# Latent attention heads: value products in high and low parts, and a new order of the work around them

## The chip, the cores and the metric

One core of a Trainium2 chip runs the whole program. The metric is device time in microseconds (us); the profile is of one execution on that core. The core's engines work from queues of their own, in order, and wait for one another on semaphores: TensorE (matmul, PE, with its weight loads as PEld), VectorE (DVE), ScalarE (ACT), GpSimd (POOL), and SyncE (SP), which issues most transfers.

## The reference, cut to what matters

A first block (a mixer with recurrence and convolution, then a feed-forward part) is followed by a second block of two attention layers. The change is in the first of these, latent attention over 512 tokens and 256 context tokens with 16 heads:

```python
q = (rms_norm(q_lat, g_qa) @ w_qb).reshape(bsz, n, A_HEADS, A_NOPE + A_ROPE)      # 64 + 32
kv = (rms_norm(kv_lat, g_kva) @ w_kvb).reshape(bsz, n, A_HEADS, A_NOPE + A_V)     # 64 + 64
q_pe, k_pe = apply_rope(q_pe, cos, sin), apply_rope(k_pe, cos, sin)
# a token attends to tokens and context, a context token to the context
s = jnp.einsum('bqhgd,bkhd->bhgqk', q, k) * scale
p = jax.nn.softmax(s, axis=-1)
o = jnp.einsum('bhgqk,bkhv->bqhgv', p, v)
out = o.reshape(gate.shape) * jax.nn.silu(gate)     # then @ out_w, residual, layer norm
```

Everything is float32.

## The kernel before

Weights come as a stream of blocks of 16 tiles (128 x 128) into two raw buffers. GpSimd's `split` (L719, L732) turns each block into a high part (type float32r, which TensorE takes in one pass) and a low part (what is left), in four parts; a product is then three passes: high x high, high x low, low x high. A raw buffer and its parts serve every second block. The activations are split in the same manner, high parts by a ScalarE copy, low parts by a VectorE subtraction.

The heads run from about 850 to 1106 us. A head has seven steps, `j` = 0 to 6: six for the 128 keys each of the 768 (scores of 512 queries), and step 6 for the context queries. In step `j` TensorE issues, in this order: from step 5 on `row` of the next head (once), the scores of the *next* step (L1394 and L1397, three passes), one product of five for the next head's maxima (`tops`, L1364, L1365, L1368), a piece of the projection of the head after next (`query` at steps 0 and 2; `key` at step 4 of even heads; `value_tokens` at steps 4 and 5 of odd heads, serving a pair), and the value product of *this* step (L1415, L1418). This last one is in plain float32, weights `Pf` by values `VV`. A block of ones beside the 64 value columns gives the softmax's sums in the other 64 rows of the same output.

VectorE takes a maximum (`top`, L2967) of each `tops` product; the next `tops` waits for it, since the output buffer is single. The five give a row that is subtracted inside the score product: `row` puts it across, ScalarE's `row_copy` writes it into `QHI`, and the next head's scores wait for it. Between the maxima VectorE has the rotary part of the query (`rope_query`, `rope_query_sum`, L2951), the low parts (`query_lo` L2955, `key_lo` L2961), and `inverse` (L2978), reciprocals of 256 columns of the sums, three for a pair of heads: one in the even, two in the odd head after the pair. GpSimd's `finish` then divides a pair's outputs (L788) and multiplies by the gate (L790), with a weight block's `split` after every second pair.

ScalarE's queue in a head: output of the head before (`output_x`, after the first exponential `output_c`), the exponentials (`weigh_keys`, L2156), the query's copy behind step 3, its high part (`query_hi`, L2125) behind step 4; in even heads the key's high parts (`key_hi`, L2131), one behind step 5 and one behind step 6, with `row_copy` between; in odd heads the values' copy at the end. In head 15 the high parts of the gated output (`out_high`, L2176) stand between the exponentials, and VectorE's `out_low` (L3018) follows. The first query product of an odd head waits for `key_lo`, as both use the output buffer `wide(2)`. Behind the heads comes the output projection (`residual_product`), which takes its eighth input only when the last pair is divided, gated and split.

Of the kernel before, what the change touches and what calls it, by code (L numbers as in the profile page):

```python
# [114 lines left out]
def build(nc, x_t, ctx_t, stream, ada_w, vectors, squares, level_masks, scan_mask, ropes, lora_w, gate_w,  # L115
# [289 lines left out]
    QHI = [reg(f"QHI{i}", [P, TA], kb, F32R) for i, kb in enumerate((136, 67, 73))]  # L405
    QLO = [reg(f"QLO{i}", [P, TA], kb, F32R) for i, kb in enumerate((139, 70, 76))]
    KHI = [[reg(f"KHI{i}{e}", [P, TA], kb + 3 * e, F32R) for e in range(2)] for i, kb in enumerate((115, 79))]
    KLO = [[reg(f"KLO{i}{e}", [P, TA], kb + 3 * e, F32R) for e in range(2)] for i, kb in enumerate((121, 85))]
    VV = [[reg(f"V{i}{e}", [P, 6, P], kb + 3 * e) for e in range(2)] for i, kb in enumerate((127, 100))]
    qf = [reg("qf0", [P, TA], 133), reg("qf1", [P, TA], 46)]  # L410
    Pf = reg("Pf", [P, 4, T], 106)
    Of = [reg("Of0", [P, TA], 91), reg("Of1", [P, TA], 40)]
# [4 lines left out]
    OT_HI = [reg(f"OT_HI{k}", [P, TA], kb, F32R) for k, kb in enumerate((49, 52, 55, 58, 61, 64, 67, 100))]  # L417
    OT_LO = [reg(f"OT_LO{k}", [P, TA], kb, F32R) for k, kb in enumerate((70, 73, 76, 79, 85, 97, 91, 103))]
    rope = at("rope", [P, 2, T], F32, tmp_at)
# [19 lines left out]
    score_full, value_done, tops_full = sem("score_full"), sem("value_done"), sem("tops_full")  # L439
    qproj_full = sem("qproj_full")  # L440
    exp_done, query_copied, query_high = sem("exp_done"), sem("query_copied"), sem("query_high")
    value_copied, ox_copied, oc_copied = sem("value_copied"), sem("ox_copied"), sem("oc_copied")
# [63 lines left out]
    def value_signal(p):  # L506

        if p == N_PAIRS - 1 or (p and p % 2 == 0):
            return block_done, pair_block(p)[0] + 1
        return vproj_full.at((p + 1) // 2 + 1 if p else 1)  # L510

    def nope_rows(e):
# [201 lines left out]
    def _(pool):  # L714
# [69 lines left out]

        def finish(p):

            pool.wait_ge(sums_inverse, 3 * p + 3)
            pool.tensor_tensor(Of[p % 2][:, :], Of[p % 2][:, :], Ls[p % 2][:, :], ALU.mult).then_inc(pair_divided, 1)  # L788
            pool.wait_ge(pair_divided, p + 1)
            pool.tensor_tensor(gate_s[:, p, :], gate_s[:, p, :], Of[p % 2][:, :], ALU.mult).then_inc(pair_out, 1)  # L790
# [11 lines left out]
        for e in range(2):  # L802
            c = slice(96, 128) if e == 0 else slice(0, 32)
            step(pool.memset(KHI[1][e][c, :].bitcast(F32), 0.0))
            step(pool.memset(KHI[1][e][top_at(e):top_at(e) + 1, :].bitcast(F32), 1.0))
            step(pool.memset(KLO[1][e][c, :].bitcast(F32), 0.0))
            step(pool.memset(VV[1][e][:, :, 64 - 64 * e:128 - 64 * e], 1.0))
        pool.sem_inc(mla_filled.sem, 1)
# [4 lines left out]

        n = before
        for p in range(N_PAIRS):
            finish(p)
            if p % 2 == 0:
                split(n, half_of(n), n // 2)
                n += 1
        if n % 2:  # L820
            split(n, 1, n // 2)
        rest, third = n + n % 2, STREAM["diff_out"] + 2
# [15 lines left out]
    def _(pe):  # L838
# [465 lines left out]
        def query(h, k):  # L1304

            p, e = h // 2, h % 2
            n, t0 = pair_block(p)
            if k == 0:
                pe.wait_ge(split_full, n + 1)
                if h == 1 or (e == 0 and h > 0):  # L1310
                    pe.wait_ge(value_copied, max(p, 1))
                if h == 2:
# [65 lines left out]
        def scores(h, j):  # L1378
# [12 lines left out]
            for k, q, first, last in ((KHI, QHI, True, False), (KHI, QLO, False, False), (KLO, QHI, False, True)):  # L1391
                kt, qq = k[p % 2][e], q[h % 3]
                if j < 6:
                    mm = pe.matmul(banks[i % 2][:, :], kt[:, P * j:P * j + P], qq[:, 0:T], start=first, stop=last)  # L1394
                else:
                    for c in range(2):
                        mm = pe.matmul(banks[i % 2][:, C * c:C * c + C], kt[:, T + P * c:T + P * c + P], qq[:, T:TA],  # L1397
                                       start=first and c == 0, stop=last and c == 1, skip_group_check=True)
            mm.then_inc(score_full, 1)

        def values(h, j):
# [12 lines left out]
            if j < 6:  # L1414
                mm = pe.matmul(pairs[1][:, 0, :], v[:, j, :], Pf[:, i % 4, :], start=(j == 0), stop=(j == 5), skip_group_check=True)  # L1415
            else:
                for c in range(2):
                    mm = pe.matmul(pairs[1][:, 1, 0:C], v[:, 4 + c, :], Pf[:, i % 4, C * c:C * c + C], start=(c == 0), stop=(c == 1),  # L1418
                                   skip_group_check=True)
# [36 lines left out]
        for h in range(A_HEADS):  # L1456
            nxt, after = h + 1, h + 2
            for j in range(N_S):
# [8 lines left out]
                if after < A_HEADS:  # L1467
# [275 lines left out]
    def _(act):  # L1743
# [391 lines left out]
        def value_copy(p):  # L2135
# [3 lines left out]
            for e in range(2):  # L2139
                c = slice(64 * e, 64 * e + 64)  # L2140
                ins = act.activation(VV[p % 2][e][:, :, c], wide(2).rearrange("p (a b) -> p a b", a=6)[:, :, c], ACT.Copy)
            ins.then_inc(value_copied, 1)
# [8 lines left out]
        def weigh_keys(h, j):  # L2151
            i = N_S * h + j
            act.wait_ge(score_full, i + 1)
            if i >= 4:
                act.wait_ge(value_done, i - 3)
            act.activation(Pf[:, i % 4, :], banks[i % 2][:, :], ACT.Exp, scale=A_SCALE).then_inc(exp_done, 1)  # L2156

        def take_output(h, n, cols, src, done):

            p, e = h // 2, h % 2  # L2160
            mine, sums = nope_rows(e), nope_rows(1 - e)
            act.wait_ge(value_done, n)
            if p >= 2:
                act.wait_ge(pair_out, p - 1)
            act.activation(Of[p % 2][mine, cols], src[mine, :], ACT.Copy)
            act.activation(Ls[p % 2][mine, cols], src[sums, :], ACT.Copy).then_inc(done, 1)
# [22 lines left out]
        for h in range(A_HEADS):  # L2189
# [14 lines left out]
            if h == A_HEADS - 1:  # L2204
                out_high(1)
            weigh_keys(h, 3)
            if h == A_HEADS - 1:
                out_high(2)
            if after < A_HEADS:
                query_copy(after)  # L2210
            weigh_keys(h, 4)
            if after < A_HEADS:
                query_hi(after)
# [3 lines left out]
            if h == A_HEADS - 1:  # L2217
                out_high(4)
            if after < A_HEADS and h % 2 == 0:
                key_hi(after // 2, 0)  # L2220
# [227 lines left out]
    def _(dve):  # L2448
# [481 lines left out]
        for e in range(2):  # L2930
            c = slice(96, 128) if e == 0 else slice(0, 32)
            dve.memset(KHI[0][e][c, :].bitcast(F32), 0.0)
            dve.memset(KLO[0][e][c, :].bitcast(F32), 0.0)
            ins = dve.memset(VV[0][e][:, :, 64 - 64 * e:128 - 64 * e], 1.0)
        chain.link(ins)
# [17 lines left out]
        def query_lo(h):  # L2953
            dve.wait_ge(query_high, h + 1)
            dve.tensor_tensor(QLO[h % 3][:, :], qf[h % 2][:, :], QHI[h % 3][:, :], ALU.subtract).then_inc(query_low, 1)  # L2955

# [25 lines left out]
        key_lo(0)  # L2982
        query_lo(0)
        rope_query(1)
        rope_query_sum(1)
# [4 lines left out]
        for h in range(A_HEADS):  # L2990
            nxt, after = h + 1, h + 2
            if nxt < A_HEADS:
                top(nxt, 0)
            if h >= 2:
                inverse((h - 2) // 2, 0 if h % 2 == 0 else 1)
            if nxt < A_HEADS:
                top(nxt, 1)
            if h >= 2 and h % 2:
                inverse((h - 2) // 2, 2)
            if nxt < A_HEADS:  # L3000
                top(nxt, 2)
            if after < A_HEADS:
# [7 lines left out]
            if after < A_HEADS:  # L3010
                query_lo(after)
                if h % 2 == 0:
                    key_lo(after // 2)
        def out_low(k):
            dve.wait_ge(ot_hi, k + 1)
            if k == KT - 1:
                dve.wait_ge(value_done, N_S * A_HEADS)
# [558 lines left out]
```

## Time and profile before

| | |
|---|---|
| median of 3 runs | 1634.55 us (1633.47 to 1636.34) |
| profiled execution | 1634.97 us, its span 1633.2 us |
| TensorE busy | 1569.9 us (96%) |
| VectorE, GpSimd, ScalarE busy | 996.3, 922.8, 695.8 us |
| granted TensorE clock, mean | 0.995 of full speed |
| heads | about 850 to 1106 us |

A matmul's recorded length is longer than the time it costs, since matmuls overlap; what one costs is the distance from its start to the next start. Behind a float32 product the records of starts run ahead, so distances are taken over a whole group.

### The profile page before, as it was taken

Reading aid. Unit: us, or ns where it says so; the run is one execution under the profiler, and the core shown is the slowest. Engines: PE = TensorE matmul, PEld = TensorE weight load, DVE = VectorE, ACT = ScalarE, POOL = GpSimd, SP = SyncE. Lnnn points to the kernel's source line nnn. Section 1 sums busy time; section 2 is a strip of 40 time slices with the busy share of each in tenths; the row PEclk is TensorE's granted clock in tenths of the full one; section 3 lists DMA queues with packets and bytes.
Section 4 is the critical chain, followed back from the end, with each engine's and each line's share of the span. In section 5 each row is a group of like instructions: output and inputs, shape, how many; then the busy total and the mean of one; then the engine's idle time right before and its main releaser. Section 6 shows DMA issues by size and latency. Waiting matters only on the chain.

```text
span 1633.2 us, 27294 instructions
## 1 busy us (share of the span) xinstructions
PE 1569.9 (96%) x11080; PEld 1272.0 (78%) x11080; DVE 996.3 (61%) x1315; ACT 695.8 (43%) x1210; POOL 922.8 (57%) x735
## 2 busy tenths in 40 slices
PE   8999888999999999989999999999999999999996
PEld 7677887678888888877877777768878888888775
DVE  6699886747555640044455766664676665666666
ACT  5552775333222220042246555563263344444563
POOL 5344887929999999965471312326624443344522
PEclk9999999999999999999999999999999999999998
DMA  6121104422332233231110000004231101111201
GB/s 206 70 103 52 55 4 159 155 104 78 103 103 84 96 141 142 103 142 69 61 58 21 27 0 27 0 1 155 84 137 52 46 33 52 52 52 52 116 40 52
DMA packets 20605, 126.08 MB, mean 77 GB/s; under 512 B 2288, under 2 KB 4592, under 8 KB 6416
## 3 DMA queue, kind: packets, MB, share of 16 engines
q1 hardware_dynamic: 20352, 124.02, 21.1%
q8 instruction: 79, 1.29, 0.3%
q10 hardware_dynamic: 144, 0.52, 0.1%
q14 instruction: 30, 0.25, 0.0%
HBM read 122.43 MB, written 2.10 MB: 76 GB/s over the span
## 4 chain that ended last, share of the span: by engine, by line
PE 77%; DVE 10%; issue 7%; ACT 3%; POOL 2%; DMA 0%; SPq 0%; POOLq 0%; ACTq 0%; DVEq 0%
PE banks L873 7%; PE banks L874 7%; PE banks L875 6%; PE banks L1415 5%; PE banks L1626 4%; PE banks L1629 4%; PE banks L1627 4%; PE banks L1394 4%; PE banks L1277 3%; PE banks L1282 3%; PE banks L1278 3%; PE banks L1249 2%; PE banks L1248 2%; PE banks L1250 2%; PE banks L1681 2%
## 5 line engine op out<-in xcount | busy, mean ns | idle before, releaser
L732 POOL TENSOR_TENSOR w_hi<-raw,der 128x512 fp32r<-128x512 f32 x296 | 333.8, 1138 | 399.9 <-PE banks L1629 203.5
L719 POOL TENSOR_TENSOR w_lo<-raw,w_hi 128x512 fp32r<-128x512 f32 x336 | 476.6, 1431 | 59.2 <-ACT w_hi L1782 58.9
L873 PE MATMUL banks<-h_hi,w_hi 128*128 128x512 f32 x464 | 184.2, 397 | 0.3 <-DVEq L2502 0.3
L874 PE MATMUL banks<-h_lo,w_hi 128*128 128x512 f32 x464 | 180.7, 389 | 0.0
L875 PE MATMUL banks<-h_hi,w_lo 128*128 128x512 f32 x464 | 180.6, 389 | 0.0
L1626 PE MATMUL banks<-h_hi,w_hi 128*128 128x512 f32 (+1 forms) x384 | 145.8, 380 | 1.3 <-DVE h_lo L3083 1.3
L1627 PE MATMUL banks<-h_lo,w_hi 128*128 128x512 f32 (+1 forms) x384 | 130.8, 355 | 0.0
L2307 ACT ACTIVATE dP<-banks,der 128x768 f32<-128x768 f32 x60 | 54.1, 902 | 159.0 <-DVE der L3181 159.0
L1629 PE MATMUL banks<-h_hi,w_lo 128*128 128x512 f32 (+1 forms) x384 | 115.9, 356 | 0.0
L788 POOL TENSOR_TENSOR Of<-Of,Ls 128x768 f32<-128x768 f32 x8 | 14.7, 1832 | 173.0 <-DVE Ls L2978 173.0
L873 PEld LDWEIGHTS banks<-h_hi,w_hi 128*128 128x128 f32 x464 | 87.1, 188 | 25.8 <-issue 7.5
L3181 DVE TENSOR_REDUCE der<-banks 128x1 f32<-128x768 f32 x64 | 60.9, 953 | 70.9 <-PE banks L1662 70.9
L874 PEld LDWEIGHTS banks<-h_lo,w_hi 128*128 128x128 f32 x464 | 87.1, 188 | 18.9 <-issue 1.4
L875 PEld LDWEIGHTS banks<-h_hi,w_lo 128*128 128x128 f32 x464 | 87.1, 188 | 18.1
L1415 PE MATMUL banks<-Pf,V 128*128 128x512 f32 x192 | 99.0, 596 | 0.7 <-ACT Pf L2156 0.4
L2967 DVE TENSOR_REDUCE nmr<-banks 128x1 fp32r<-128x768 f32 x64 | 60.5, 945 | 60.1 <-PE banks L1365 59.3
L1277 PE MATMUL banks<-h_hi,w_hi 128*128 128x512 f32 x248 | 89.1, 359 | 8.3 <-DVE h_lo L2877 5.7
L2156 ACT ACTIVATE Pf<-banks 128x512 f32<-128x512 f32 x112 | 66.5, 595 | 57.1 <-PE banks L1394 55.3
L1626 PEld LDWEIGHTS banks<-h_hi,w_hi 128*128 128x128 f32 x384 | 72.3, 188 | 17.5 <-DVE h_lo L3083 2.1
L1278 PE MATMUL banks<-h_lo,w_hi 128*128 128x512 f32 x248 | 82.2, 349 | 0.0
L1627 PEld LDWEIGHTS banks<-h_lo,w_hi 128*128 128x128 f32 x384 | 72.5, 189 | 10.3 <-issue 1.9
L1394 PE MATMUL banks<-QHI,KHI 128*128 128x512 f32 x96 | 71.9, 749 | 0.0
(551 smaller groups left out, 3853.5 us busy)
## 6 DMA issues: line engine op xcount, KB each, us to landing
raw<-in_stream SPq DMA_DIRECT2D x83, 1024.0 KB, 4.8
ada_home<-in_ada_w SPq DMA_DIRECT2D x18, 1024.0 KB, 7.4
xT<-in_x_t SPq DMA_DIRECT2D x4, 512.0 KB, 7.6
raw<-in_ada_w SPq DMA_DIRECT2D x2, 1024.0 KB, 4.8
xT<-in_x_t SPq DMA_DIRECT2D x1, 2048.0 KB, 7.5
ada_late_home<-in_ada_w SPq DMA_DIRECT2D x2, 1024.0 KB, 5.8
ada_end<-in_ada_w SPq DMA_DIRECT2D x2, 1024.0 KB, 9.9
out_t<-z SPq DMA_DIRECT2D x16, 128.0 KB, 1.7
```

What stands on the lines that cost most here:

```text
L719: return pool.tensor_tensor(lo[:, h, part(i), :], raw_tiles(half)[:, part(i), :], hi[:, h, part(i), :], ALU.subtract)
L732: pool.tensor_tensor(hi[:, h, part(i), :], raw_tiles(half)[:, part(i), :], one, ALU.mult).then_inc(hi_done, 1)
L873: pe.matmul(banks[b][:, :], hi, tile(rhs_hi, k), start=(at_k == 0), stop=False)
L874: pe.matmul(banks[b][:, :], hi, tile(rhs_lo, k), start=False, stop=False)
L875: mm = pe.matmul(banks[b][:, :], lo, tile(rhs_hi, k), start=False, stop=(at_k == KT - 1))
L1277: pe.matmul(out, hi, cols(rhs_hi, k0 + k, a, b), start=(k == 0), stop=False)
L1278: pe.matmul(out, hi, cols(rhs_lo, k0 + k, a, b), start=False, stop=False)
L1394: mm = pe.matmul(banks[i % 2][:, :], kt[:, P * j:P * j + P], qq[:, 0:T], start=first, stop=last)
L1415: mm = pe.matmul(pairs[1][:, 0, :], v[:, j, :], Pf[:, i % 4, :], start=(j == 0), stop=(j == 5), skip_group_check=True)
L1626: pe.matmul(out, hi, h2_hi[:, k, a:b], start=(k == 0), stop=False)
L1627: pe.matmul(out, hi, h2_lo[:, k, a:b], start=False, stop=False)
L1629: mm = pe.matmul(out, lo, h2_hi[:, k, a:b], start=False, stop=(k == KT - 1))
```

## The change

Heads 1 to 15 take the value products of steps 2 to 6 in parts. ScalarE writes `P_high` (float32r) from `Pf` (`weights_high`), GpSimd writes `P_low`, their difference (`weigh_low`); the values of tiles 2 to 5 are kept as `VHI` (with the ones) and `VLO` (64 columns, from VectorE's new `value_lo`). TensorE then issues three passes in place of the float32 product. Steps 0 and 1, and head 0, stay in float32. Around this:

- every value product stands one step later in TensorE's queue; `Pf` has three buffers in place of four, `QLO` two in place of three (so `query_lo` also waits for the scores of the head two before);
- in VectorE's queue `inverse` stands one maximum later: the first behind maximum 1, the second behind maximum 2;
- in ScalarE's queue `row_copy` stands ahead of both `key_hi`, which come behind the exponential of step 6;
- GpSimd splits two blocks in parts at the start of heads 4 to 11 and a third in heads 12 to 14; the fourth comes behind the last head, ahead of the last pair's divide and gate multiply. Those of the other pairs stand behind the first and second `weigh_low` of odd heads;
- the ones are in columns 64 to 128 for both heads of a pair, so outputs always come from the lower 64 rows.

```diff
+        def weigh_low(h, j):
+            m, i = low_index(h, j), N_S * h + j
+            pool.wait_ge(*p_high.at(m + 1))
+            pool.tensor_tensor(P_low[m % 2][:, :], Pf[:, i % 3, :], high_home(h, j)[:, :], ALU.subtract).then_inc(p_low.sem, 1)
...
+        for h in range(1, A_HEADS):
...
+            for block_n, i in parts_of.get(h, ()):
+                split_part(block_n, i)
+            for j in range(FIRST_LOW, N_S):
+                weigh_low(h, j)
+                if h >= 3 and h % 2 and j == FIRST_LOW:
+                    divide((h - 3) // 2)
+                if h >= 3 and h % 2 and j == FIRST_LOW + 1:
+                    gate_out((h - 3) // 2)
+        for i in range(PARTS):
+            split_part(before + 3, i)
+        divide(N_PAIRS - 1)
+        gate_out(N_PAIRS - 1)
...
-            pe.wait_ge(exp_done, i + 1)
-            v = VV[p % 2][e]
...
+                high = high_home(h, j)
+                pe.wait_ge(*p_high.at(low_index(h, j) + 1))
...
+                for c, (tile, cols) in enumerate(pairs_of):
+                    pe.matmul(out, high_v[:, tile - FIRST_LOW, :], high[:, cols], start=begins and c == 0, stop=False, skip_group_check=True)
+                    pe.matmul(out[0:64, :], VLO[p % 2][e][:, tile - FIRST_LOW, :], high[:, cols], start=False, stop=False, skip_group_check=True)
+                pe.wait_ge(*p_low.at(low_index(h, j) + 1))
+                for c, (tile, cols) in enumerate(pairs_of):
+                    mm = pe.matmul(out, high_v[:, tile - FIRST_LOW, :], P_low[low_index(h, j) % 2][:, cols], start=False, stop=ends and c == len(pairs_of) - 1,
...
-                values(h, j)
+                if j:
+                    values(h, j - 1)
+                elif h:
+                    values(h - 1, N_S - 1)
+        values(A_HEADS - 1, N_S - 1)
...
+        def weights_high(h, j):
+            i = N_S * h + j
+            if in_parts(h, j):
+                m = low_index(h, j)
+                act.wait_ge(exp_done, i + 1)
+                if m >= 2:
+                    act.wait_ge(value_done, read_by(m - 2))
+                act.activation(high_home(h, j)[:, :], Pf[:, i % 3, :], ACT.Copy).then_inc(p_high.sem, 1)
...
+            weights_high(h, 5)
             if nxt < A_HEADS:
                 row_copy(nxt)
             weigh_keys(h, 6)
             if after < A_HEADS:
                 if h % 2 == 0:
-                    key_hi(after // 2, 1)
+                    for e in range(2):
+                        key_hi(after // 2, e)
                 else:
                     value_copy(after // 2)
+            weights_high(h, 6)
...
             if nxt < A_HEADS:
                 top(nxt, 0)
+                top(nxt, 1)
             if h >= 2:
                 inverse((h - 2) // 2, 0 if h % 2 == 0 else 1)
             if nxt < A_HEADS:
-                top(nxt, 1)
+                top(nxt, 2)
             if h >= 2 and h % 2:
                 inverse((h - 2) // 2, 2)
-            if nxt < A_HEADS:
-                top(nxt, 2)
             if after < A_HEADS:
                 rope_query(after)
```

## Rows read from the trace of the kernel before

**Rows 1.** The page, part 1: busy time of each engine, share of the span, instructions.

```profile
PE 1569.9 (96%) x11080; PEld 1272.0 (78%) x11080; DVE 996.3 (61%) x1315; ACT 695.8 (43%) x1210; POOL 922.8 (57%) x735
```

**Rows 2.** Windows of heads 4, 5, 14, 15: length, PE, PEld, DVE, ACT, POOL busy; clock.

```profile
914.01:930.09 16.08, 16.08 (x77) 11.62 (x75) 9.73 (x11) 10.30 (x18) 7.04 (x7) 1.00 0.20 65
930.09:947.47 17.38, 17.28 (x88) 12.73 (x87) 12.55 (x13) 9.48 (x18) 3.65 (x2) 1.00 0.00 1
1081.31:1095.22 13.91, 13.53 (x59) 8.71 (x57) 9.40 (x8) 6.88 (x13) 0.05 (x1) 1.00 0.01 2
1095.22:1106.08 10.86, 10.60 (x40) 6.40 (x38) 7.51 (x5) 9.71 (x18) 10.78 (x7) 1.00 0.00 0
```

**Rows 3.** Timeline, head 5: start, length; a value product, then score passes.

```profile
934.61 1.02 PE L1415 MATMUL banks<-Pf,V 128*128 128x512 f32 x2
...
935.70 0.39 PE L1394 MATMUL banks<-QLO,KHI 128*128 128x512 f32 x1
...
935.92 0.39 PE L1394 MATMUL banks<-QHI,KLO 128*128 128x512 f32 x1
```

**Rows 4.** Groups by line, heads 1 to 14: busy us, mean ns | idle before.

```profile
L2156 ACT ACTIVATE Pf<-banks 128x512 f32<-128x512 f32 x94 | 55.9, 595 | 52.6 <-PE banks L1394 51.4
...
L719 POOL TENSOR_TENSOR w_lo<-raw,w_hi 128x512 fp32r<-128x512 f32 x12 | 15.3, 1283 | 0.0
...
L788 POOL TENSOR_TENSOR Of<-Of,Ls 128x768 f32<-128x768 f32 x6 | 11.0, 1831 | 149.8 <-DVE Ls L2978 149.8
L2125 ACT ACTIVATE QHI<-qf 128x768 fp32r<-128x768 f32 x13 | 11.0, 845 | 22.3 <-DVE qf L2951 22.3
```

**Rows 5.** Timeline, head 5, VectorE, and the last maximum product on TensorE.

```profile
932.50 1.75 DVE L2978 RECIPROCAL Ls<-Ls 128x256 f32<-128x256 f32 x1
...
934.81 0.96 DVE L2967 TENSOR_REDUCE nmr<-banks 128x1 fp32r<-128x768 f32 x1 [0.55 <-PE banks L1365]
...
935.68 1.74 DVE L2978 RECIPROCAL Ls<-Ls 128x256 f32<-128x256 f32 x1
...
937.34 0.90 DVE L2967 TENSOR_REDUCE nmr<-banks 128x1 fp32r<-128x768 f32 x1
...
939.68 0.96 DVE L2967 TENSOR_REDUCE nmr<-banks 128x1 fp32r<-128x768 f32 x1
...
941.01 0.40 PE L1368 MATMUL banks<-KHI,QHI 128*128 128x256 f32 x2
```

**Rows 6.** Timeline, head 14: a maximum, and the next maximum product.

```profile
1085.83 0.90 DVE L2967 TENSOR_REDUCE nmr<-banks 128x1 fp32r<-128x768 f32 x1
...
1086.78 0.50 PE L1364 MATMUL banks<-KHI,QHI 128*128 128x512 f32 x1 [0.33 <-DVE nmr L2967]
```

**Rows 7.** Timeline, head 4 into 5: from the last maximum product to the query.

```profile
924.59 0.40 PE L1368 MATMUL banks<-KHI,QHI 128*128 128x256 f32 x2
...
924.99 0.84 ACT L2125 ACTIVATE QHI<-qf 128x768 fp32r<-128x768 f32 x1 [1.51 <-DVE qf L2951]
...
928.05 0.60 ACT L2156 ACTIVATE Pf<-banks 128x512 f32<-128x512 f32 x1
...
928.67 0.81 ACT L2131 ACTIVATE KHI<-banks 64x768 fp32r<-64x768 f32 x1
...
929.51 1.93 DVE L2961 TENSOR_TENSOR KLO<-banks,KHI 64x768 fp32r<-64x768 f32 x2 [2.69 <-ACT KHI L2131]
...
931.58 0.47 PE L1277 MATMUL banks<-lat_hi,w_hi 128*128 128x512 f32 x1
```

**Rows 8.** Timeline, head 15 and the output projection: output's low parts, a split.

```profile
1098.46 8.35 DVE L3018 TENSOR_TENSOR OT_LO<-gate_s,OT_HI 128x768 fp32r<-128x768 f32 x5 [3.37 <-ACT OT_HI L2176]
...
1102.29 1.99 POOL L719 TENSOR_TENSOR w_lo<-raw,w_hi 128x512 fp32r<-128x512 f32 x1
...
1119.92 0.96 DVE L3018 TENSOR_TENSOR OT_LO<-gate_s,OT_HI 128x768 fp32r<-128x768 f32 x1 [4.76 <-ACT OT_HI L2176]
...
1121.02 0.40 PE L1277 MATMUL banks<-OT_HI,w_hi 128*128 128x512 f32 x1
```

More of the change, by code:

```diff
@@ L510, in value_signal, with in_parts, low_index, read_by @@
         return vproj_full.at((p + 1) // 2 + 1 if p else 1)
+    def in_parts(h, j):
+        return h > 0 and j >= FIRST_LOW
+    def low_index(h, j):
+        return LOWS * (h - 1) + j - FIRST_LOW
+    def read_by(m):
+        return N_S * (m // LOWS + 1) + FIRST_LOW + m % LOWS + 1
+    def high_home(h, j):
+        return P_high[1 if h >= A_HEADS - 2 else 0][low_index(h, j) % 2]
+    def whole_values(h):
+        return VF[h // 2 % 2][h % 2] if h else V_first
+    def value_tiles(p):
+        return wide(2).rearrange("p (a b) -> p a b", a=6)
     def nope_rows(e):
@@ L783, in _, with divide, gate_out @@
                 split(2 * i + (second + s), s, i + second // 2)
-        def finish(p):
+        def divide(p):
             pool.wait_ge(sums_inverse, 3 * p + 3)
             pool.tensor_tensor(Of[p % 2][:, :], Of[p % 2][:, :], Ls[p % 2][:, :], ALU.mult).then_inc(pair_divided, 1)
+        def gate_out(p):
             pool.wait_ge(pair_divided, p + 1)
@@ L806, in _ @@
             step(pool.memset(KLO[1][e][c, :].bitcast(F32), 0.0))
-            step(pool.memset(VV[1][e][:, :, 64 - 64 * e:128 - 64 * e], 1.0))
+            step(pool.memset(VF[1][e][:, :, 64:128], 1.0))
+            step(pool.memset(VHI[1][e][:, :, 64:128].bitcast(F32), 1.0))
         pool.sem_inc(mla_filled.sem, 1)
@@ L812, in _, with split_part @@
         pool.sem_inc(kpe_low.sem, 1)
[L814 to L821, printed above, removed]
+        def split_part(n, i):
+            half, m = half_of(n), n - (N_IN - 1)
+            if i == 0:
+                pool.wait_ge(raw_full[half], 16 * (n // 2 + 1))
+                pool.wait_ge(block_done, n - 1)
+            pool.tensor_tensor(w_hi[:, half, part(i), :], raw_tiles(half)[:, part(i), :], one, ALU.mult).then_inc(hi_done, 1)
+            pool.wait_ge(hi_done, PARTS * m + i + 1)
+            low_of(half, half, i).then_inc(quarter_split if i < PARTS - 1 else split_full, 1)
+        def weigh_low(h, j):
+            m, i = low_index(h, j), N_S * h + j
+            pool.wait_ge(*p_high.at(m + 1))
+            pool.tensor_tensor(P_low[m % 2][:, :], Pf[:, i % 3, :], high_home(h, j)[:, :], ALU.subtract).then_inc(p_low.sem, 1)
+        n = before + 4
+        parts_of = {h: [(before + (h - 4) // PARTS, (h - 4) % PARTS)] for h in range(4, 12)}
+        parts_of[12] = [(before + 2, 0), (before + 2, 1)]
+        parts_of[13] = [(before + 2, 2)]
+        parts_of[14] = [(before + 2, 3)]
+        for h in range(1, A_HEADS):
+            if h == 2:
+                pool.wait_ge(value_done, N_S)
+                pool.memset(VF[0][0][:, :, 64:128], 1.0)
+                pool.memset(VHI[0][0][:, :, 64:128].bitcast(F32), 1.0)
+            for block_n, i in parts_of.get(h, ()):
[10 more added lines that the diff above has]
+        gate_out(N_PAIRS - 1)
         rest, third = n + n % 2, STREAM["diff_out"] + 2
@@ L1411, in values @@
                 pe.wait_ge(oc_copied, h)
-            pe.wait_ge(exp_done, i + 1)
-            v = VV[p % 2][e]
-            if j < 6:
-                mm = pe.matmul(pairs[1][:, 0, :], v[:, j, :], Pf[:, i % 4, :], start=(j == 0), stop=(j == 5), skip_group_check=True)
-            else:
-                for c in range(2):
-                    mm = pe.matmul(pairs[1][:, 1, 0:C], v[:, 4 + c, :], Pf[:, i % 4, C * c:C * c + C], start=(c == 0), stop=(c == 1),
+            v, high_v, pairs_of = whole_values(h), VHI[p % 2][e], ((j, slice(0, T)),) if j < 6 else ((4, slice(0, C)), (5, slice(C, 2 * C)))
+            out, n = (pairs[1][:, 0, :], T) if j < 6 else (pairs[1][:, 1, 0:C], C)
+            begins, ends = (j == 0, j == 5) if j < 6 else (True, True)
+            if not in_parts(h, j):
+                pe.wait_ge(exp_done, i + 1)
+                for c, (tile, cols) in enumerate(pairs_of):
+                    mm = pe.matmul(out, v[:, tile, :], Pf[:, i % 3, cols], start=begins and c == 0, stop=ends and c == len(pairs_of) - 1,
+                                   skip_group_check=True)
+            else:
+                high = high_home(h, j)
+                pe.wait_ge(*p_high.at(low_index(h, j) + 1))
+                if j == FIRST_LOW:
+                    pe.wait_ge(*value_low.at(p + 1))
+                for c, (tile, cols) in enumerate(pairs_of):
+                    pe.matmul(out, high_v[:, tile - FIRST_LOW, :], high[:, cols], start=begins and c == 0, stop=False, skip_group_check=True)
+                    pe.matmul(out[0:64, :], VLO[p % 2][e][:, tile - FIRST_LOW, :], high[:, cols], start=False, stop=False, skip_group_check=True)
+                pe.wait_ge(*p_low.at(low_index(h, j) + 1))
+                for c, (tile, cols) in enumerate(pairs_of):
+                    mm = pe.matmul(out, high_v[:, tile - FIRST_LOW, :], P_low[low_index(h, j) % 2][:, cols], start=False, stop=ends and c == len(pairs_of) - 1,
                                    skip_group_check=True)
@@ L2139, in value_copy @@
             for e in range(2):
-                c = slice(64 * e, 64 * e + 64)
-                ins = act.activation(VV[p % 2][e][:, :, c], wide(2).rearrange("p (a b) -> p a b", a=6)[:, :, c], ACT.Copy)
+                c, whole = slice(64 * e, 64 * e + 64), FIRST_LOW if p or e else 6
+                ins = act.activation(whole_values(2 * p + e)[:, 0:whole, 0:64], value_tiles(p)[:, 0:whole, c], ACT.Copy)
+                if whole < 6:
+                    ins = act.activation(VHI[p % 2][e][:, :, 0:64], value_tiles(p)[:, whole:6, c], ACT.Copy)
             ins.then_inc(value_copied, 1)
@@ L2164, in take_output @@
                 act.wait_ge(pair_out, p - 1)
-            act.activation(Of[p % 2][mine, cols], src[mine, :], ACT.Copy)
+            act.activation(Of[p % 2][mine, cols], src[values, :], ACT.Copy)
             act.activation(Ls[p % 2][mine, cols], src[sums, :], ACT.Copy).then_inc(done, 1)
@@ L2954, in query_lo, with value_lo @@
             dve.wait_ge(query_high, h + 1)
-            dve.tensor_tensor(QLO[h % 3][:, :], qf[h % 2][:, :], QHI[h % 3][:, :], ALU.subtract).then_inc(query_low, 1)
+            if h >= 2:
+                dve.wait_ge(score_full, N_S * (h - 1))
+            dve.tensor_tensor(QLO[h % 2][:, :], qf[h % 2][:, :], QHI[h % 3][:, :], ALU.subtract).then_inc(query_low, 1)
+        def value_lo(p):
+            dve.wait_ge(value_copied, p + 1)
+            if p >= 2:
+                dve.wait_ge(value_done, N_S * (2 * p - 2))
+            for e in range(0 if p else 1, 2):
+                c = slice(64 * e, 64 * e + 64)
+                ins = dve.tensor_tensor(VLO[p % 2][e][:, :, :], value_tiles(p)[:, 2:6, c], VHI[p % 2][e][:, :, 0:64], ALU.subtract)
+            ins.then_inc(value_low.sem, 1)
         def key_lo(p):
@@ L2983, in _ @@
         query_lo(0)
+        value_lo(0)
         rope_query(1)
@@ L3010, in _ @@
             if after < A_HEADS:
-                query_lo(after)
-                if h % 2 == 0:
+                if h % 2:
+                    query_lo(after)
+                    value_lo(after // 2)
+                else:
+                    query_lo(after)
                     key_lo(after // 2)
@@ L3015, in out_low @@
             dve.wait_ge(ot_hi, k + 1)
+            if k == 0:
+                dve.wait_ge(value_done, N_S * (A_HEADS - 1))
             if k == KT - 1:
```

40 lines of the change are left out of this document (28 added, 12 removed).

## The prediction

> **What bounds the kernel now.** I read the page first: TensorE is busy for 96% of the span, no other engine for more than 61% [rows 1]. Next came the windows of single heads. An even head takes 16.08 us and an odd one 17.38, TensorE is busy for all but 0.1 us of either, and the granted clock is 1.00, so at the higher of its two levels; ScalarE works 10.30 and VectorE 12.55 us at most in such a head [rows 2]. So in the heads matmul time sets the pace, and the others matter only by the time at which their results arrive. The last two heads, which prepare no later one, are looser: 13.53 of 13.91 us and 10.60 of 10.86 [rows 2]. The timeline then gives the prices and, above all, how closely VectorE and ScalarE keep ahead of TensorE.
>
> **Value products.** Two fp32 instructions of 512 columns and the first fp32r one behind them take from 934.61 to 935.70, 1.09 us; the next fp32r one takes 0.23 [rows 3]. So an fp32 value product costs 0.86 us, and three fp32r passes 0.70 (the score products, also three passes, show it). The context step has twice the instructions at half the columns and comes to the same. Parts are used for steps 2 to 6 of heads 1 to 15: 75 x 0.16 = **-12.0 us**. I take no gain from passes with 64 output rows: the columns stream all the same.
>
> **New work beside it.** Each such step adds one ScalarE copy of 512 columns (not in the trace; bounds 0.60, the exponential of the same size, and 0.84, a 768-column copy [rows 4]; I take 0.60, the row of its size) and one GpSimd subtraction of 512 columns (1.28 us, as the weights' low part [rows 4]). Per head ScalarE goes from 10.3 to 13.3 us of about 15.3, GpSimd to 6.4 plus a divide and gate multiply (1.83 each, every second head) and 2.3 for one part of a split: at most 12.4. Both fit, and the values come one step later, which leaves 3.4 us or more between a score and its value product, against 0.2 + 0.60 + 0.60 + 1.28 = 2.7 for exponential, copy and subtraction. In the middle heads I cost this at nothing. The ring of three for the weights costs nothing either: the third-last product is issued ahead of the score. Memsets, value_lo (about 0.9 us, VectorE idle there) and the split parts among the heads: nothing, their consumers are several us away. The moved places of buffers: nothing.
>
> **Reciprocals a maximum later.** Before, in an odd head, VectorE runs maximum 0, reciprocal, maximum 1 (934.81), reciprocal (935.68), maximum 2 (937.34 to 938.24), the two rotary products, maximum 3 (939.68 to 940.64), and TensorE needs that one for the last maximum product at 941.01: 0.37 us to spare [rows 5]. The first reciprocal stood in the gap in which VectorE waited for product 1. Now both come behind maximum 1. From the end of maximum product 1, VectorE needs 0.20 + 0.96 + 1.75 + 0.96 + 1.75 + 1.44 + 0.96 = 8.0 us to the end of maximum 3 (0.20 is the hand-over, 1.44 the stretch from 938.24 to 939.68). Passes are priced by columns, 0.23 for 512 and 0.12 for 256 (so 0.35 for a maximum product, 1.05 for half a query or a key, some 0.06 for each of the six of a row). TensorE needs, in order, value 0.86, score 0.70, product 2 0.35, query 1.05, value 0.86, score 0.70, product 3 0.35, value 0.70, score 0.70 = 6.3. It waits 1.7 us in heads 3, 5, ..., 13, the six that have two reciprocals: **+10.2 us**. That such a wait is real is seen in head 14 before, where a reciprocal holds back a maximum to 1085.83 and TensorE stands idle for 0.33 us ahead of the next product [rows 6]. It comes on top of the key's wait below, since this chain starts behind it. An even head has one reciprocal: 6.3 us of VectorE against 6.3, no wait worth counting.
>
> **The row's copy in front of the key's.** Before, in an even head, from the last maximum product (924.59): the query's high part ends at 925.83, then exponential, first key copy, row copy, exponential (928.05), second key copy (928.67), key's low parts (929.51 to 931.44), and TensorE's query of the next head starts at 931.58, 0.3 us late and 7.0 us behind the start [rows 7]. Now: 1.24 to the query's high part and 0.3 for maximum 3, which comes just in time (1.6), exponential 0.6, high part 0.6, row copy 0.8, exponential 0.6, both key copies 1.6, low parts 1.93, steps between them 0.2: 7.9. TensorE reaches that query after its product 0.23, key 1.05, three values 2.1, row 0.36, three scores 2.1 and the next head's first product 0.35 = 6.2. Wait 1.7 against 0.3: +1.4 for heads 2, 4, ..., 12, six times 8.4. In head 0, without high parts, the chain from the last score is 0.8 + 1.6 + 1.93 + 0.1 = 4.4 against 3.5 on TensorE: 0.9 against 0.3, +0.6. Together **+9.0 us**. The row copy itself, behind the new high part, ends some 0.2 us after TensorE wants the next head's first score: 6 x 0.2 = **+1.2**. At the end of odd heads value_copy and value_lo end within 0.2 us of need: nothing.
>
> **Head 15 and what follows.** Here is no query or maximum work to cover the chain. ScalarE had 9.71 us [rows 2]; five copies more are 12.7. By order, with 0.38 for 256 columns: output 1.4, exponential 2.0, context output 2.8, first output copy 3.6, exponential 4.2, second copy and high part 2 at 5.6 us from the head's start, its low part at 6.95, and then GpSimd has divide (1.83), low 3, gate multiply (1.83), low 4, low 5, low 6, at 1.28 each, with small waits: 15.8. The last product ends at about 16.0, against 10.86 before. Its 0.8 of the gain is counted above, so **+6.1**. The last split, four parts of 2.3 us, now stands between low 6 and the last divide; the divide starts 10.5 us after the heads, and with 1.83 + 1.83 + 0.85 + 0.96 and hand-overs the last low part is there at 16.1. Before, it ended at 1120.88 and TensorE took it at 1121.02, 14.9 us after the heads [rows 2, 8]. **+1.4**. Covers that keep this from being more: fourteen product groups of the output projection, 14.7 us. The loads of the queue on SP are released by signals that shift with it.
>
> **Sum.** -12.0 + 10.2 + 9.0 + 1.2 + 6.1 + 1.4 = +15.9. The profiled execution took 1634.97 us (span 1633.2 and 1.8 outside), 0.4 above the median. 1634.97 + 15.9 = 1650.9: I say **1651 us**, 1.0% slower. What a measurement can tell from no change is about 0.2%, 3.3 us.
>
> **A rule against the change.** VectorE's subtraction of the output's low part, both inputs in SBUF, takes 1.67 us a piece where GpSimd works (8.35 for five), and GpSimd's subtraction then 1.99 [rows 8] where it takes 1.28 on its own [rows 4]. The Trainium skill (SBUF — State Buffer, "Who interferes with whom") says that a VectorE instruction with two SBUF inputs and a GpSimd one that reads SBUF exclude each other for the whole instruction. By that rule the trace agrees. My sum has 1.28 throughout; if five low parts of head 15 take 1.99, that is 5 x 0.7 = +3.5, and the rotary sum right behind maximum 3 can meet a low part, up to 1.28 in each of heads 2 to 13: at most +15.
>
> **The rivals.**
> 1. *Both waits and the tail, as summed*: 1651, range 1644 to 1659. For it: the spare of 0.37 and the wait of 0.3 that stand there already. Chance 0.62.
> 2. *One of the two waits hardly comes.* The key's chain would be shorter by 1 us if ScalarE, which waits for the rotary sum, catches up: 8.4 less gives 1642.5; the same for the reciprocals gives 1640.7. Against it: each queue is served in order. Chance 0.13.
> 3. *Faster: the reciprocals and keys stay covered.* The mechanism is that a product waits for the maximum before it, and the delayed score step leaves more TensorE work in that gap than I count. It decides below 0.75 us of new wait per pair of heads (12.0 less the 7.5 of the tail, over six); at none the time is 1634.97 - 12.0 + 7.5 = 1630.5. For it: ScalarE and VectorE have 2 us or more idle per head. Against it: 8.0 against 6.3. Chance 0.13.
> 4. *GpSimd becomes the bound by shared reads*: an odd head with a split part would have 2.33 + 5 x 1.99 + 3.66 = 15.9 us, and low parts come late: 1660 to 1668. For it [rows 8]; against it, VectorE's maxima and reciprocals, most of its work, have one input at most from SBUF. Chance 0.12.
>
> Range for 8 in 10: 1637 to 1666. Rival 3 falls outside, the others in. Faster by over 0.2%: 0.11; within it 0.06; slower 0.83.
>
> **What would show it.** Right: heads of 15.5 (even) and 19.6 us (odd); idle TensorE of some 1.7 us ahead of the last maximum product of odd heads, released by VectorE's maximum, and of some 1.7 ahead of the first query product of odd heads, released by KLO; head 15 of 16 us; GpSimd's last divide behind eight split instructions. Wrong: odd heads under 18 us, or waits ahead of value products in the middle heads. The forecast fails if the copies are much longer than 0.6, if a low part arrives late, or if the reciprocals find the gap after all.

## The result, and the profile after

The changed kernel takes 1653.18 us (median of 4 runs, 1652.6 to 1653.8) against 1635.44 (4 runs, 1633.47 to 1636.77): a ratio of 1.0104, 95% interval 1.009 to 1.0117. It is 17.7 us slower. The forecast was 16 more, 1651 us in a range of 1637 to 1666.

The page's first part after the change, to be put beside [rows 1]:

```profile
PE 1571.2 (95%) x11170; PEld 1284.4 (78%) x11170; DVE 1010.2 (61%) x1331; ACT 741.4 (45%) x1300; POOL 1025.0 (62%) x814
```

The span grew by 18.8 us (1633.2 to 1652.0), 18.2 of it between head 0's maxima and the last input of the output projection. TensorE's busy time grew by only 1.3. So the cheaper products were eaten by time in which TensorE does nothing, or works at a lower clock. Where that is, the windows tell. First two stretches of the kernel before, from one last maximum product to the next but one (a pair of heads), and from that of head 14 to the end of the heads:

```profile
907.95:941.41 33.46, 33.36 (x162) 24.35 (x162) 22.28 (x24) 19.78 (x34) 12.65 (x10) 1.00 0.10 33
1091.09:1106.08 14.99, 14.73 (x62) 9.10 (x60) 11.48 (x8) 11.95 (x21) 10.83 (x7) 1.00 0.00 0
```

The same after the change: two pairs, a piece of the second of them, the stretch from head 13's to head 14's last maximum product, the end of the heads with its last part, and the output projection up to its last input. Columns as in [rows 2]: length, busy time of PE, PEld, DVE, ACT, POOL, then the granted clock.

```profile
943.82:978.79 34.97, 32.30 (x174) 24.94 (x173) 24.42 (x26) 25.80 (x46) 22.23 (x17) 1.00 0.09 31
978.79:1015.02 36.23, 33.59 (x174) 26.59 (x173) 24.63 (x26) 25.92 (x46) 21.47 (x17) 0.95 0.00 1
980.30:984.00 3.70, 3.70 (x22) 3.54 (x21) 1.23 (x2) 2.81 (x5) 3.54 (x3) 0.54 0.02 4
1084.95:1101.03 16.08, 16.01 (x83) 12.67 (x82) 9.15 (x10) 11.76 (x23) 11.24 (x10) 0.89 0.00 0
1101.03:1123.69 22.66, 17.70 (x74) 11.84 (x73) 10.26 (x8) 16.46 (x28) 16.67 (x11) 0.85 0.00 1
1116.40:1123.70 7.30, 6.05 (x20) 4.16 (x21) 0.80 (x1) 3.04 (x5) 6.88 (x5) 0.54 0.00 1
1123.69:1139.49 15.80, 15.19 (x86) 12.80 (x85) 8.21 (x8) 9.16 (x14) 13.48 (x10) 1.00 0.52 199
```

A pair of heads went from 33.46 to 34.97 us, 1.5 more; forecast was 1.7 more. One pair took 36.23 with the same work: for some 3.4 us of it the granted clock is at half (0.54 over the window that holds them). The end of the heads went from 15.0 to 22.7, the output projection's first stretch from 14.94 [rows 2, 8] to 15.80.

By single heads, cut as in [rows 2], head 4 takes 15.32 us and head 5 19.64, where the prediction named 15.5 and 19.6; head 15 takes 18.63 where it named 16:

```profile
915.06:930.38 15.32, 15.32 (x82) 11.95 (x81) 9.79 (x10) 11.85 (x21) 8.53 (x7) 1.00 0.00 1
930.38:950.02 19.64, 16.96 (x93) 12.99 (x92) 14.62 (x15) 13.95 (x27) 13.69 (x10) 1.00 0.00 0
1105.06:1123.69 18.63, 13.76 (x50) 8.91 (x49) 6.32 (x6) 12.96 (x23) 13.75 (x9) 0.82 0.01 1
```

In the waits between heads 1 and 14 (us in total, times, longest) TensorE is named with releasers that it had hardly before:

```profile
PEld banks L1433 <- DVE nmr L3078: 11.4, 6, 1.9
PE banks L1433 <- DVE nmr L3078: 8.8, 6, 1.5
PE banks L1341 <- DVE KLO L3072: 7.9, 7, 1.2
PEld banks L1495 <- POOL P_low L862: 2.1, 4, 0.5
```

L1433 is the last maximum product, in the six heads that were named; L1341 the query behind the key, in seven. L1495 is a value product that waits for its low part, in four heads. The timeline of head 5 shows the first of them, to be read against [rows 5]:

```profile
935.82 0.96 DVE L3078 TENSOR_REDUCE nmr<-banks 128x1 fp32r<-128x768 f32 x1 [2.22 <-PE banks L1430]
936.81 1.75 DVE L3089 RECIPROCAL Ls<-Ls 128x256 f32<-128x256 f32 x1
...
938.48 0.90 DVE L3078 TENSOR_REDUCE nmr<-banks 128x1 fp32r<-128x768 f32 x1
939.29 1.74 DVE L3089 RECIPROCAL Ls<-Ls 128x256 f32<-128x256 f32 x1
...
942.47 0.96 DVE L3078 TENSOR_REDUCE nmr<-banks 128x1 fp32r<-128x768 f32 x1
943.48 0.51 PE L1433 MATMUL banks<-KHI,QHI 128*128 128x256 f32 x2 [1.46 <-DVE nmr L3078]
```

VectorE is idle for 2.22 us ahead of maximum 1, where a reciprocal of 1.75 had stood, and then works without a pause up to maximum 3, which TensorE awaits.

### The profile page after: what moved, and what is told of

It reads as the page before. It is cut to its first block, busy times and chain, and to the rows that moved or that the text cites. A ratio compares the mean times of both kernels' runs of the same rounds, so it can differ in the third digit from the quotient of the medians.

```text
span 1652.0 us, 27769 instructions
## 1 busy us (share of the span) xinstructions
PE 1571.2 (95%) x11170; PEld 1284.4 (78%) x11170; DVE 1010.2 (61%) x1331; ACT 741.4 (45%) x1300; POOL 1025.0 (62%) x814
## 4 chain that ended last, share of the span: by engine, by line
PE 72%; DVE 11%; issue 8%; POOL 4%; ACT 4%; DMA 1%; SPq 0%; ACTq 0%; POOLq 0%; DVEq 0%
PE banks L937 7%; PE banks L938 6%; PE banks L939 6%; PE banks L1707 4%; PE banks L1710 4%; PE banks L1708 4%; PE banks L1341 3%; PE banks L1346 3%; PE banks L1342 2%; PE banks L1314 2%; PE banks L1312 2%; PE banks L1313 2%; PE banks L1762 2%; PE banks L1459 2%; PE banks L1742 2%
## 5 line engine op out<-in xcount | busy, mean ns | idle before, releaser
L764 POOL TENSOR_TENSOR w_hi<-raw,der 128x512 fp32r<-128x512 f32 x280 | 315.2, 1136 | 388.4 <-PE banks L1710 203.6
L939 PE MATMUL banks<-h_hi,w_lo 128*128 128x512 f32 x464 | 180.6, 389 | 0.0
L862 POOL TENSOR_TENSOR P_low<-Pf,P_high 128x512 fp32r<-128x512 f32 x75 | 100.6, 1346 | 84.1 <-ACT P_high L2248 83.8
L938 PEld LDWEIGHTS banks<-h_lo,w_hi 128*128 128x128 f32 x464 | 87.1, 188 | 18.8 <-issue 1.4
L1341 PE MATMUL banks<-h_hi,w_hi 128*128 128x512 f32 x248 | 89.2, 360 | 6.8 <-DVE h_lo L2973 4.2
L1346 PE MATMUL banks<-h_hi,w_lo 128*128 128x512 f32 x248 | 71.2, 350 | 0.0
L1313 PE MATMUL banks<-act_lo,w_hi 128*128 128x512 f32 x176 | 68.5, 389 | 0.0
```

The lines of the kernel that those rows point to most:

```text
L764: pool.tensor_tensor(hi[:, h, part(i), :], raw_tiles(half)[:, part(i), :], one, ALU.mult).then_inc(hi_done, 1)
L938: pe.matmul(banks[b][:, :], hi, tile(rhs_lo, k), start=False, stop=False)
L939: mm = pe.matmul(banks[b][:, :], lo, tile(rhs_hi, k), start=False, stop=(at_k == KT - 1))
L1313: pe.matmul(b[:, :], hi, act_lo[:, k, :], start=False, stop=False)
L1341: pe.matmul(out, hi, cols(rhs_hi, k0 + k, a, b), start=(k == 0), stop=False)
L1346: mm = pe.matmul(pairs[w][:, a // 512, 0:b - a], lo, cols(rhs_hi, k0 + k, a, b), start=False, stop=(k == kn - 1))
```

## The experiments

The first four each undo or change one thing in the changed kernel (1653.2 us). The second four build on what they showed. Times are medians of 4 to 12 executions, ratios are to the kernel before the change, timed beside them: its median was 1635.7 us beside the first four and 1636.4 beside the second, so a difference between times of the two sets can be off by about 1 us.

**The reciprocals back.** Only in odd heads:

```diff
             if nxt < A_HEADS:
                 top(nxt, 0)
+            if h >= 2 and h % 2:
+                inverse((h - 2) // 2, 1)
+            if nxt < A_HEADS:
                 top(nxt, 1)
             if h >= 2:
-                inverse((h - 2) // 2, 0 if h % 2 == 0 else 1)
+                inverse((h - 2) // 2, 0 if h % 2 == 0 else 2)
             if nxt < A_HEADS:
                 top(nxt, 2)
-            if h >= 2 and h % 2:
-                inverse((h - 2) // 2, 2)
```

> Only the odd heads' two reciprocals go back to where they stood before (behind maximum 0 and behind maximum 1); all else is as in the changed kernel. Theory A, VectorE's order: the changed kernel shows TensorE idle for 1.46 us ahead of the last maximum product in heads 3, 5, ..., 13; these six waits shrink to about 0.1, which saves 8 to 9 us, and the stretch of half clock in head 7 behind such a wait (1.3 us lost) may go too: 1641 to 1645 us against 1653.2. Theory B, GpSimd: low part 3 of an odd head stands behind the divide and becomes the next thing that is late, so that at most 3 us are won: 1650 or more.

Measured: 1643.24 us, ratio to the kernel before the change 1.0045 (1.0031 to 1.0059). 9.9 us won, the wait at L1433 is gone from the list: theory A. But a smaller one has come, ahead of the row (L1440). So a pair takes 33.85 us, only 1.1 less than 34.97; the rest of the gain in the heads is the lower clock, which no middle head has in this trace. The list of waits and the timeline of head 5:

```profile
PE banks L1440 <- DVE nmr L3080: 4.4, 6, 0.7
```

```profile
939.23 1.84 POOL L824 TENSOR_TENSOR gate_s<-gate_s,Of 128x768 f32<-128x768 f32 x1
939.37 2.25 DVE L3051 TENSOR_TENSOR qf<-qf,otmp 32x512 f32<-32x512 f32 x1
...
942.39 0.52 PE L1440 MATMUL banks<-ident_r,nmr 128*1 128x128 f32 x6 [0.74 <-DVE nmr L3080]
```

VectorE's rotary sum, 0.68 us on its own, takes 2.25 when GpSimd's gate multiply has begun 0.14 us ahead of it. In the changed kernel it takes 1.25 in the same heads, beside a low part.

**The exponential of step 5 ahead of the query's high part.**

```diff
+            weigh_keys(h, 5)
             if after < A_HEADS:
                 query_hi(after)
...
-            weigh_keys(h, 5)
```

> In ScalarE's queue the exponential of step 5 goes ahead of the query's high part, which waits for the rotary sum. Theory A, the key's chain is ScalarE's queue from the rotary sum on: it loses up to one exponential, 0.6 us, so the wait of 1.18 us for KLO at the start of odd heads falls to about 0.6 in heads 5 to 13 and 3: 2 to 4 us saved, 1649 to 1651. Theory B, the wait for KLO comes from VectorE or from the shared reads with GpSimd: no change, 1652.5 to 1654.

Measured: 1652.68 us, 1.0107 (1.0092 to 1.0122). No gain that can be told, and the wait for KLO is what it was, 7.9 us in seven. But theory B's reason is not the right one either. The timeline of heads 6 and 7 says where the 0.6 us went:

```profile
961.63 0.84 ACT L2206 ACTIVATE QHI<-qf 128x768 fp32r<-128x768 f32 x1
...
963.19 0.63 ACT L2248 ACTIVATE P_high<-Pf 128x512 fp32r<-128x512 f32 x1 [0.71 <-PE banks L1495]
...
968.60 0.47 PE L1341 MATMUL banks<-lat_hi,w_hi 128*128 128x512 f32 x1 [1.17 <-DVE KLO L3072]
```

ScalarE now comes to high part 5 earlier and stands there for 0.71 us (0.28 in the changed kernel), until TensorE has done value product 3: the two `P_high` buffers alternate. So the chain to KLO is anchored in value product 3, not in the rotary sum. From 963.19 on, high part, row copy, exponential, two key copies and low parts run to 968.45 almost without a gap.

**The first key copy back in front of the row's.**

```diff
             weights_high(h, 5)
+            if after < A_HEADS and h % 2 == 0:
+                key_hi(after // 2, 0)
             if nxt < A_HEADS:
                 row_copy(nxt)
...
-                    for e in range(2):
-                        key_hi(after // 2, e)
+                    key_hi(after // 2, 1)
```

> The first key copy goes back in front of the row's copy. Theory A, what counts is the sum of the work in the chain and not its order: TensorE waits some 0.8 us for the row at the next head's first score and that much less for KLO: 1652 to 1655. Theory B, the row's copy in front is what keeps the wait small: without it the waits add up, 7 x 0.8 = 5.6 us more, 1657 to 1660.

Measured: 1653.01 us, 1.0102 (1.0086 to 1.0117). Theory A. The waits show the trade, the row's (L1459) against the key's:

```profile
PE banks L1341 <- DVE KLO L3073: 3.0, 6, 0.5
PE banks L1459 <- ACT QHI L2232: 2.8, 5, 0.6
```

Whether the row's copy stands in front of the key's, as in the change, therefore makes no difference that can be told.

**Head 15 in float32.**

```diff
-        return h > 0 and j >= FIRST_LOW
+        return 0 < h < A_HEADS - 1 and j >= FIRST_LOW
```

and the values of its tiles 2 to 5, with ones, in a float32 buffer of their own.

> Head 15 keeps its value products in float32 as before the change (no high and low weights there); all other heads as in the changed kernel. Theory A, the chain of copy and subtraction without cover is what makes the end of the heads long: the stretch from the last maximum product of head 14 to the output projection falls from 22.7 us to 15 to 16: 1645 to 1647. Theory B, the order of the products (one step later) and the ring of three are the cause: at most 3 us less, 1650 or more.

Measured: 1646.32 us, 1.0057 (1.0043 to 1.007), 6.9 less. Theory A. The window from head 14's last maximum product to the output projection, 22.66 us above, is:

```profile
1104.90:1119.60 14.70, 14.61 (x68) 9.98 (x67) 11.21 (x7) 12.80 (x22) 13.36 (x9) 1.00 0.01 2
```

**The gate multiply one low part later**, on top of the reciprocals back:

```diff
-                if h >= 3 and h % 2 and j == FIRST_LOW + 1:
+                if h >= 3 and h % 2 and j == FIRST_LOW + 2:
                     gate_out((h - 3) // 2)
```

> The reciprocals as in the run before (1643.2 us), and GpSimd's gate multiply of a pair one low part later. In that run the rotary sum of odd heads (two inputs in SBUF) takes 2.25 us instead of 0.68 while GpSimd's gate multiply runs, the last maximum comes late, and TensorE is idle for 0.74 us ahead of the row in six heads. Theory A, the two engines exclude each other on the read side: with the multiply moved away the sum is back near 0.7 and the six waits go: 3 to 4.5 us less, 1638.5 to 1640.5. Theory B, the sum is slow for another reason, or the low part that takes the multiply's place collides in the same way: 1642 to 1644.

Measured: 1638.85 us, 1.0012 (1.0 to 1.0024), 4.4 less. Theory A: the rotary sum is at 0.68 us in every head from 1 on, and the six waits at the row are gone. Head 5:

```profile
939.85 0.68 DVE L3051 TENSOR_TENSOR qf<-qf,otmp 32x512 f32<-32x512 f32 x1
```

**The first key copy by VectorE**, on top of these. ScalarE keeps `key_hi(p, 1)`:

```diff
+        def first_key(p):
+            r = nope_rows(0)
...
+            dve.tensor_copy(KHI[p % 2][0][r, :], wide(2)[r, :]).then_inc(key_low.sem, 1)
+            dve.wait_ge(*key_low.at(2 * p))
+            dve.tensor_tensor(KLO[p % 2][0][r, :], wide(2)[r, :], KHI[p % 2][0][r, :], ALU.subtract)
...
                 else:
+                    first_key(after // 2)
                     query_lo(after)
                     key_lo(after // 2)
```

> As the one before, and of the two key copies the first is made by VectorE, right behind the last maximum of even heads, with its low part at once; ScalarE copies only the second. Theory A, the wait for KLO (1.2 us in seven heads) is the length of the chain from value product 3 over high part, row copy, exponential and two key copies to the low parts: it is 1.8 us shorter and the wait goes: 7 to 9 us less than the one before, 1630 to 1633. Theory B, VectorE's extra copy delays the maxima instead: less than 3 us.

Measured: 1630.39 us, 0.9964 (0.9951 to 0.9978), 8.5 less; its twelve executions scatter from 1625.9 to 1635.2. Theory A. This is the first one faster than the kernel before. What TensorE still waits for, above all, is head 15's low parts:

```profile
PE banks L1497 <- POOL P_low L862: 4.4, 3, 2.8
```

**All of it**: the one before, head 15 in float32, and the last pair's divide and gate multiply ahead of the last quarter of the last split.

> The one before, with head 15 in float32 (7 us by itself) and the last pair's divide and gate multiply ahead of the last quarter of the last split (about 1 us). Theory A, the losses of the change are separate waits and add up: 1630 to 1633 less 8 gives 1622 to 1626, that is 10 to 13 us below the kernel before the change, which is what the 60 to 75 cheaper value products are worth. Theory B, with one wait gone the next takes its place: 1628 or more.

Measured: 1623.10 us, 0.9915 (0.990 to 0.9931), 7.3 less than the one before. Theory A. What the order in the tail gives by itself was not measured. The same three stretches as above: a pair of heads, the end of the heads, the output projection:

```profile
903.51:935.03 31.52, 31.52 (x174) 25.10 (x174) 24.15 (x27) 25.22 (x45) 22.00 (x17) 1.00 0.01 1
1075.32:1090.40 15.08, 14.98 (x70) 10.36 (x70) 11.22 (x7) 13.17 (x23) 13.47 (x9) 1.00 0.01 2
1090.40:1105.50 15.10, 14.08 (x80) 12.07 (x79) 10.34 (x9) 9.86 (x16) 9.84 (x7) 1.00 0.53 208
```

In the pair TensorE is busy for all 31.52 us. Against 33.46 that is 1.94 less: ten products at 0.16, and the 0.3 by which the key's chain was late before [rows 7].

**The first key copy by VectorE, alone** in the changed kernel:

> The changed kernel with the first key copy made by VectorE, nothing else. Theory A: the waits for KLO go and the six waits for the maximum stay, 1653.2 less 8 is 1644 to 1647. Theory B, the two kinds of wait trade against each other, since the odd heads' VectorE chain starts earlier: 1650 or more.

Measured: 1645.52 us, 1.0057 (1.0039 to 1.0076), 7.7 less. Theory A: the list has no wait for KLO any more and the other as it was.

```profile
PE banks L1435 <- DVE nmr L3088: 8.8, 6, 1.5
```

The losses are separate. From 1653.2, the reciprocals with the gate multiply moved gave 14.3 (9.9, and 4.4 on top), the key copy alone 7.7, head 15 alone 6.9, together 28.9; all of them and the tail's order in one kernel gave 30.1. The 4.4 were measured on top of the reciprocals only: the collision of sum and multiply is not in the changed kernel.

## Why the prediction was right, step by step

The time is 2 us below the measured one, and the two large waits came where they were forecast and nearly as long. That it came so close is in part luck. From head 0's to head 14's last maximum product the trace has 9.7 us more, where the terms for these heads add up to 9.2; but key and row were put 3.2 us too high there, and the lower clock (2.5) and a late low part (1.2) were left out. The end of the heads was put 2.9 us too low. The terms:

**Value products, -12.0.** Right. In the kernel with all edits a pair of heads is 1.94 us shorter than before the change, of which 1.6 are ten products at 0.16.

**Reciprocals, +10.2.** Right. The idle time is 1.46 us in each of the six heads, 8.8 in all. From start to start, as the forecast counts, the loss is 1.63 (the last score pass starts at 941.62, the maximum product at 943.48, and a pass costs 0.23), 9.8 in all. That undoing it gave 9.9 is not the same sum: a pair got 1.1 shorter, as the wait ahead of the row came in, which is 6.7 in six, and the lower clock of heads 7 and 13 went, another 2.5. The 8.0 us that were added up for VectorE came out a little shorter: from maximum 1 (935.82) to the end of maximum 3 (943.43) are 7.6 us, 7.8 with the hand-over. One thing was missed, though it only shows once the reciprocals are back: the rotary sum meets the gate multiply, and TensorE waits 0.74 us a time. The paragraph on the rule had a low part in that place, which is what the changed kernel has (1.25 us in the six odd heads).

**Key's chain, +9.0, and row, +1.2.** The key's is right in its place, a fifth too large. The idle time is 1.2 us a head, 7.9 in all. From start to start, the query came 1.45 us behind the product before it (966.27 to 967.72) where it had been 0.38 (931.20 to 931.58): 1.07 more in six heads, and 0.6 in head 0, make 7.0. Making the chain shorter gave 7.7, as it also takes away the 0.3 a head that were there before. The row's own wait, 0.2, did not come. The heading under which I put it was the wrong one: the order of row and key makes no difference that can be told (1653.0 against 1653.2). The chain is long because a high part has been put into it and the ring of two starts it at value product 3. That anchor I had passed over, and the second experiment's miss showed it.

**Head 15, +6.1, undersized.** From head 14's last maximum product to the end the stretch grew by 7.7 us, the forecast (3.8 + 16.0 against 4.1 + 10.9) had 4.8. (By the prediction's own numbers, 16.0 - 10.86 + 0.8, the term is 5.9 and not 6.1.) GpSimd's instructions were priced at 1.28 and 1.83; the timeline has:

```profile
1111.91 2.54 POOL L820 TENSOR_TENSOR Of<-Of,Ls 128x768 f32<-128x768 f32 x1
...
1114.41 1.98 POOL L862 TENSOR_TENSOR P_low<-Pf,P_high 128x512 fp32r<-128x512 f32 x1
1116.35 2.54 POOL L824 TENSOR_TENSOR gate_s<-gate_s,Of 128x768 f32<-128x768 f32 x1
1116.44 0.50 PE L1495 MATMUL banks<-P_low,VHI 128*128 128x512 f32 x1 [2.78 <-POOL P_low L862]
```

They run in part beside VectorE's output low parts, and TensorE waits 2.78 us for the low part of step 3, and 0.88 and 1.20 for two others. That is 0.7 + 0.7 + 0.7 = 2.1 us in the chain. The prediction's paragraph on the rule gave a bound of +3.5, but for low parts alone; here divide and multiply are two of the three. The Trainium skill (SBUF — State Buffer, "Who interferes with whom") has this as an exclusion for the whole instruction. The first and the fifth experiment agree: the rotary sum takes 2.25 us beside GpSimd's multiply and ends 0.55 after it, and 0.68 apart from it. Behind the wait of 2.78 the clock fell to half for the last 6.8 us of the head, which no term had, but this cost little. In the second and third experiments, with the same queues in head 15 and less of the lower clock, the stretch is only 0.3 and 0.5 us shorter. The other 0.3 to 0.5 us of the 2.9 are not explained.

**Tail, +1.4.** A little too large: measured 0.86, with 0.42 us of idle time at the last input:

```profile
1138.47 0.96 DVE L3135 TENSOR_TENSOR OT_LO<-gate_s,OT_HI 128x768 fp32r<-128x768 f32 x1 [6.47 <-ACT OT_HI L2268]
...
1139.49 0.51 PE L1341 MATMUL banks<-OT_HI,w_hi 128*128 128x512 f32 x1 [0.42 <-DVE OT_LO L3135]
```

**New work costed at nothing.** Nearly right for the middle heads: the copies take 0.632 us (median of 75) where 0.60 was taken, the subtractions 1.29 where 1.28 was, and the rival in which GpSimd becomes the bound did not come there. But the value product of step 5 waits for its low part in heads 3, 5, 9 and 11 (the weight load for 0.51 us), behind a gate multiply of 2.30 us and low parts slowed in the same way; that delays TensorE by 0.3 a time, 1.2 in all. The prediction had named such waits as a sign that it is wrong, and costed them at nothing. The rival on the faster side fails at its own threshold, since the new wait per pair was 2.6 us and not below 0.75. But it was right that the engines had room: with a queue order that uses it, and head 15 left in float32, nearly the same arithmetic wins 12 to 13 us (1623.1 against 1635.4 and 1636.4).

**What the sum left out** is the lower clock. In the pair with head 7 it cost 1.26 us (36.23 against 34.97). Behind head 13's wait it cost 1.2: the stretch to head 14's last maximum product takes 16.08 us there, and 14.9 in the second and third experiments, which keep the order of these heads and have the full clock. The second experiment's:

```profile
1085.90:1100.79 14.89, 14.78 (x83) 11.26 (x82) 9.26 (x10) 11.21 (x22) 12.00 (x10) 1.00 0.00 0
```

In head 15, where GpSimd sets the pace, it is the 0.3 to 0.5 above.

Not tried: a third buffer for the high parts, which would loosen the chain's anchor, and high and low parts in head 15 with its output copies moved out of the way.

## What to carry to other kernels

When a saturated engine is made faster, walk every result it waits for against the new pace: here slacks of 0.4 us and less stood in the profile, and two of them, 1.6 and 1.1 us a pair, turned a gain of 1.6 into a loss. An instruction moved later in an in-order queue leaves the gap that it filled and joins the stretch that was full, so nearly its whole length counts (1.63 us of 1.75 here). And a new stage between two engines needs cover by other work; in the last unit of a loop, where that work ends, it may be better to leave the old way in place (6.9 us here).

## What was not expected of the hardware

In the heads, the granted clock of TensorE went to its lower level, 1.2 GHz, in three stretches behind waits. In head 7 TensorE was idle for 1.46 us up to 978.44, worked at full clock until 980.4, and then for 3.4 us at half, with a queue that was full. The same wait of 1.46 us in heads 3, 5, 9 and 11 had no such consequence; in head 13 it had, and in head 15 behind 2.78 us. The windows ahead of, in and behind the stretch in head 7:

```profile
976.30:978.40 2.10, 0.68 (x3) 0.20 (x2) 2.04 (x3) 0.63 (x1) 2.10 (x2) 1.00 0.00 0
978.40:980.40 2.00, 1.96 (x14) 1.68 (x14) 1.95 (x2) 0.64 (x1) 2.00 (x2) 1.00 0.00 0
980.40:983.80 3.40, 3.40 (x21) 3.34 (x19) 0.93 (x1) 2.71 (x5) 3.40 (x3) 0.50 0.02 5
983.80:986.20 2.40, 2.40 (x13) 1.96 (x13) 1.61 (x3) 1.87 (x6) 0.33 (x2) 0.99 0.00 0
```

So a wait can cost more than its length. The five kernels with the wait of 1.46 us in six heads show it again: each of their traces has two or three such stretches in the middle heads, 12 behind 30 waits, and each begins one to two us behind a wait. In the five without it (before, and the first, fifth, sixth and seventh experiments) the clock is 1.00 in all middle heads, though two of these have the wait of 1.2 us for the key. What decides whether a wait is followed by a stretch is not shown.
